# A two-block transformer forward pass on one core: moving modulation work, key casts, one early expert block and the table's side products

## What is computed

```python
def first_block(x, mem, ...):       # layer 0: h @ l0_w_in ("even_in"), mixers, @ l0_w_out ("even_out")
    ...                             # layer 1: h @ l1_w_in ("odd_in"), mixers, @ l1_w_out ("odd_out")

def second_block(x, c, ...):
    for l in range(DEPTH):                                     # DEPTH = 2
        mod = (silu(c) @ ada_w[l] + ada_b[l])[:, None, :]      # 6 * 1024 values
        sh1, sc1, g1, sh2, sc2, g2 = jnp.split(mod, 6, axis=-1)
        h = rmsnorm(x, norm_mix_g[l]) * (1.0 + sc1) + sh1
        y = rglru_block(h, ...) if l == 0 else mla_block(h, ...)
        x = x + g1 * y
        h = rmsnorm(x, norm_ffn_g[l]) * (1.0 + sc2) + sh2
        x = x + g2 * peer(h, peer_w_q[l], peer_sub_keys[l], peer_u[l], peer_v[l])

def peer(h, w_q, sub_keys, u_tab, v_tab):                      # 8 heads, 128 * 128 experts
    q = (h @ w_q).reshape(B, S, 8, 2, -1)
    s = einsum('bshpd,hpnd->bshpn', q, sub_keys)
    v1, i1 = top_k(s[..., 0, :], 16);  v2, i2 = top_k(s[..., 1, :], 16)
    cv, ci = top_k(all 16 * 16 sums of v1 and v2, 16)
    idx = i1[ci // 16] * 128 + i2[ci % 16];  g = softmax(cv)
    act = gelu(h . u_tab[idx]);  return sum(g * act * v_tab[idx])
```

## Time and profile before

| | before |
|---|---|
| median of 3 runs | 2448.44 us (2446.98 to 2449.4) |
| profiled execution | 2445.76 us, span 2444.5 us, mean granted clock of PE 0.992 |
| PE, PEld | 2355.5 us (96%), 1923.0 us (79%) |
| DVE, ACT, POOL | 1914.9 us (78%), 1164.6 us (48%), 154.2 us (6%) |
| `even_in` products begin | 45.54 us |
| `odd_out` second half, up to the next stage's first transposes | 425 to 446 us |
| routing of layer 0, DVE's last instruction | 662.95 us |
| table of layer 0, first and last store on ACT | 670.59 us, 755.73 us |

### The profile page before, as it was taken

One profiled execution on the slowest core, in us unless ns is written; L12 is line 12 of the kernel. 1 busy time (PEld: TensorE's weight loads), 2 busy tenths in 40 slices (PEclk: granted clock), 3 DMA queues, 4 the chain that ended last, 5 costly groups with the idle time before them and its releaser, 6 DMA issues. The chain is left out here.

```text
span 2444.5 us, 37915 instructions
## 1 busy us (share of the span) xinstructions
PE 2355.5 (96%) x11759; PEld 1923.0 (79%) x11759; DVE 1914.9 (78%) x4354; ACT 1164.6 (48%) x2035; POOL 154.2 (6%) x172
## 2 busy tenths in 40 slices
PE   7999999999999999999999999999899999999997
PEld 5776466778787888888888877788788888888886
DVE  5677788857997788888888867699877777777776
ACT  5674247242286544444444446316744444444443
POOL 1000000000351000000000000015400000000000
PEclk9999999999999999999999999999999999999999
DMA  7524640653213677777677751311155555555553
GB/s 257 190 102 137 236 170 5 236 197 132 78 36 122 231 252 257 253 253 260 252 253 255 257 187 70 127 63 53 62 193 191 192 193 190 190 189 189 189 189 138
DMA packets 144614, 429.31 MB, mean 176 GB/s; under 512 B 15230, under 2 KB 21374, under 8 KB 144510
## 3 DMA queue, kind: packets, MB, share of 16 engines
q1 hardware_dynamic: 144510, 428.08, 50.0%
HBM read 426.99 MB, written 1.05 MB: 175 GB/s over the span
## 5 line engine op out<-in xcount | busy, mean ns | idle before, releaser
L3405 PE MATMUL bank<-v_parts,weighted_high 128*128 128x512 f32 x1952 | 528.7, 392 | 0.5 <-DVE weighted_low L3548 0.5
L3391 PE MATMUL bank<-h_t_parts,u_t_high 128*128 128x512 f32 x1824 | 450.6, 389 | 0.0
L3405 PEld LDWEIGHTS bank<-v_parts,weighted_high 128*128 128x128 f32 x1952 | 351.1, 189 | 65.6 <-issue 2.6
L3391 PEld LDWEIGHTS bank<-h_t_parts,u_t_high 128*128 128x128 f32 x1824 | 342.3, 188 | 71.3 <-DVE u_t_low L3523 0.3
L3469 ACT ACTIVATE u_t_high<-u_ring 128x1024 fp32r<-128x1024 f32 x228 | 242.0, 1061 | 179.6 <-DMA u_ring<-in_peer_u 178.0
L3488 ACT ACTIVATE activated<-activated 128x256 f32<-128x256 f32 x228 | 95.6, 419 | 474.1 <-DVE activated L3536 474.1
L3523 DVE TENSOR_TENSOR u_t_low<-u_ring,u_t_high 128x1024 fp32r<-128x1024 f32 x228 | 278.7, 1222 | 29.4 <-ACT u_t_high L3469 26.6
L3405 PE MATMUL bank<-v_parts,weighted_low 128*128 128x512 f32 x976 | 301.5, 390 | 0.0
L3530 DVE TENSOR_TENSOR v_parts<-v_ring,v_parts 128x1024 fp32r<-128x1024 f32 x242 | 294.4, 1216 | 3.3 <-ACT v_parts L3476 3.3
L3476 ACT ACTIVATE v_parts<-v_ring 128x1024 fp32r<-128x1024 f32 x242 | 255.1, 1054 | 52.5 <-PE bank L3405 51.7
L3394 PEld LDWEIGHTS bank<-h_t_parts,u_t_low 128*128 128x128 f32 x1824 | 248.8, 190 | 17.8
(11 more groups left out here) (600 smaller groups left out, 3579.8 us busy)
## 6 DMA issues: line engine op xcount, KB each, us to landing
v_ring<-in_peer_v SPq DMA_DIRECT2D x244, 512.0 KB, 3.4
u_ring<-in_peer_u SPq DMA_DIRECT2D x228, 512.0 KB, 4.6
panel<-in_l_w_in SPq DMA_DIRECT2D x15, 2048.0 KB, 8.2
late_tiles<-in_ada_w SPq DMA_DIRECT2D x54, 512.0 KB, 4.3
mod_ring<-in_ada_w SPq DMA_DIRECT2D x42, 512.0 KB, 4.6
panel<-in_peer_w_q SPq DMA_DIRECT2D x8, 2048.0 KB, 7.8
panel<-in_l_w_out SPq DMA_DIRECT2D x4, 2560.0 KB, 10.2
early_u<-in_peer_u SPq DMA_DIRECT2D x20, 512.0 KB, 3.3
```

The lines of the kernel that those rows point to most:

```text
L3391: nc.tensor.matmul(banks[2 + k][:, :], UTH[:, k, j, :], H2[:, j, :, :].rearrange("p a s -> p (a s)"), start=(j == 0), stop=False, skip_gro ...
L3405: last = nc.tensor.matmul(banks[4 + 2 * t + half][:, :], w[:, t * P:(t + 1) * P], v[k][:, half * 512:(half + 1) * 512], start=opens and n ...
```

## The change

1. `even_in`: the first slice isn't split. PE multiplies it unsplit, without the two dummy products before it, and ACT and DVE begin with the second slice.
2. `odd_out`: `mod_steps` becomes (0, 0). Its eight modulation adds go to the end of the LRU stage, behind the second scans and the two `GROW` copies, which move there as well; their loads stand on SP between the second and third output panels. `DIAG` is made after `decays(0)`, and PE's row product stands behind `("gel", 2)`.
3. Routing, both layers: the eight casts of key numbers go from DVE to ACT (`copy_keys`); ACT's list has head h's after the scores of head h + 2, head 6's before the early blocks' copies, head 7's after four of these. POOL waits for the cast on ACT. The tenth early block's products and copy leave the stage (its load stays).
4. Table, both layers: the tenth early block's eight products stand at the head instead of the two dummy products; the 32 side products are spread over 48 steps (none, one, one); in every fourth step POOL makes token 2's one-hot too and DVE doesn't; ACT is fully unrolled, with the copy of the V tile at step 60.

The diff, cut:

```diff
@@ even_in, DVE and ACT (w_high, w_low now count from slice 1) @@
+                    if q:
+                        dve.wait_ge(w_high, q)
...
@@ even_in, PE @@
-                keep_streaming(acc_bank(g0), 2)
...
+                    if q == 0:
+                        wait_panel(pe, ps[0])
+                        for t in range(NT):
+                            last = nc.tensor.matmul(acc_bank(g0 + t)[:, :], HT[:, 0, t * P:(t + 1) * P], slots[ps[0] % 3][:, 0:512],
+                                                    start=True, stop=False)
+                        last.then_inc(used, 1)
+                        continue
@@ odd_out @@
-                     at_dve={0: dve_gated, 1: dve_mean, 2: dve_scale, 4: dve_conv}, mod_steps=(0, 16), plain=2)
+                     at_dve={0: dve_gated, 1: dve_mean, 2: dve_scale, 4: dve_conv}, mod_steps=(0, 0), plain=2)
@@ LRU stage, SP @@
                 modulation.load(sp, 6)
+                load_panels(sp, outs[1] + 1)
+                modulation.load(sp, 16)
                 load_panels(sp, outs[1] + 3)
@@ LRU stage, PE @@
-                    if job == ("rec", 0):
+                    if job == ("gel", 2):
                         pe.wait_ge(diag_ready, 1)
@@ LRU stage, DVE (MOD add and DIAG: from the start to behind decays(0)) @@
                 states(1)
+                for i in range(2):
+                    dve.wait_ge(row_ready, i + 1)
+                    f(v.tensor_copy(GROW[:, i * 512:(i + 1) * 512], banks[4 + i][:, :]), row_stored, wait=False)
+                modulation.add(f, dve, 16)
                 gain_work([(1, sc2, C("norm_ffn_g_2", 0, 8))], 24, 40)(f)
@@ routing @@
+                        if n == ROUTED - 1:
+                            break
...
+                    def copy_keys(h):
+                        act.wait_ge(keys_done, h + 1)
+                        nc.scalar.activation(IDF[:, h, :, :, :].rearrange("p i t k -> p (i t k)"),
+                                             IDX[:, h, :, :, :].rearrange("p i t k -> p (i t k)"), ACT.Copy).then_inc(keys_copied, 1)
...
+                        if g >= 2:
+                            copy_keys(g - 2)
+                    copy_keys(H - 2)
                     for n in range(ROUTED - 2):
+                        if n == 4:
+                            copy_keys(H - 1)
                         copy_early(n)
@@ table @@
+            POOL_TWO = 1
+            spread = KD * (EARLY - ROUTED)
+            last_step = 3 * S // 16
+            early_in = lambda n: n * spread // last_step
...
-                        for u in range(ACT_TOKENS, POOL_TOKEN):
+                        for u in range(ACT_TOKENS, ACT_TOKENS if s == POOL_TWO else POOL_TOKEN):
...
-                        pe.wait_ge(pool_hot, n + 1)
+                        pe.wait_ge(pool_hot, n + 1 + (n + R4 - POOL_TWO) // R4)
...
-                    keep_streaming(banks[7], 2)
+                    for k in range(KD):
+                        last = nc.tensor.matmul(banks[7][:, 0:S], UE[:, head % 3, k * P:(k + 1) * P], HT[:, k, :],
+                                                start=(k == 0), stop=(k == KD - 1))
+                    last.then_inc(head_acted, 1)
```

More of the change, by code:

```diff
@@ L1873, in _ @@
                         wait_used(act, q - 4)
-                    w = slots[ps[i] % 3][:, k * 512:(k + 1) * 512]
-                    nc.scalar.activation(ring[:, q % 4, 0, :], w, ACT.Copy).then_inc(w_high, 1)
+                    if q:
+                        w = slots[ps[i] % 3][:, k * 512:(k + 1) * 512]
+                        nc.scalar.activation(ring[:, q % 4, 0, :], w, ACT.Copy).then_inc(w_high, 1)
                     if k == 2 and i > 0:
@@ L2814, in _ @@
                 conv(0)
-                for i in range(2):
-                    dve.wait_ge(row_ready, i + 1)
-                    f(v.tensor_copy(GROW[:, i * 512:(i + 1) * 512], banks[4 + i][:, :]), row_stored, wait=False)
                 modulation.add(f, dve, 4)
@@ L2826, in _ @@
                 modulation.add(f, dve, 2)
+                f(v.tensor_tensor(MOD[:, 16:24], MOD[:, 16:24], C("ada_b_2", 16, 8), ALU.add))
+                f(v.tensor_tensor(DIAG[:, :, :], ident[:, :].unsqueeze(1).broadcast_to([P, KD, P]),
+                                  g1.unsqueeze(2).broadcast_to([P, KD, P]), ALU.mult), diag_ready)
                 mults(0)
@@ L2971, in _ @@
                     f(nc.scalar.activation(gates, gates, ACT.Exp), exp_out)
-                    for n in range(ROUTED - 2, ROUTED):
-                        copy_early(n)
+                    copy_early(ROUTED - 2)
                 @block.gpsimd
@@ L3102, in _ @@
                             done["cand"] = issued_so_far()
-                        if keys:
-                            dve.wait_ge(dve_order, done["keys"])
-                            dve.wait_ge(keys_done, h + 1)
-                            f(v.tensor_copy(IDF[:, h, :, :, :].rearrange("p i t k -> p (i t k)"),
-                                            IDX[:, h, :, :, :].rearrange("p i t k -> p (i t k)")), wait=False)
-                            done["keys"] = issued_so_far()
                         if h >= 4:
@@ L3169, in peer @@
             table_acted, table_copied = sem(f"peer{l}_table_acted"), sem(f"peer{l}_table_copied")
+            head_acted, head_copied = sem(f"peer{l}_head_acted"), sem(f"peer{l}_head_copied")
+            head = ROUTED - 1
             ACT_TOKENS = 2
             POOL_TOKEN = 3
+            POOL_TWO = 1
+            spread = KD * (EARLY - ROUTED)
+            last_step = 3 * S // 16
+            early_in = lambda n: n * spread // last_step
+            early_end = [next(n for n in range(last_step) if early_in(n + 1) == KD * (b + 1)) for b in range(EARLY - ROUTED)]
             def at_least(eng, s, value):
@@ L3202, in step @@
                         tok = slice(4 * n, 4 * n + 4) if type(n) is int else bass.ds(4 * n, 4)
-                        nc.vector.tensor_tensor(O2[:, s, :, :], rows.broadcast_to([P, 4, P]),
-                                                slot_e2[:, tok].unsqueeze(2).broadcast_to([P, 4, P]), ALU.is_equal)
-                        for u in range(ACT_TOKENS, POOL_TOKEN):
+                        last = nc.vector.tensor_tensor(O2[:, s, :, :], rows.broadcast_to([P, 4, P]),
+                                                       slot_e2[:, tok].unsqueeze(2).broadcast_to([P, 4, P]), ALU.is_equal)
+                        for u in range(ACT_TOKENS, ACT_TOKENS if s == POOL_TWO else POOL_TOKEN):
                             last = nc.vector.tensor_scalar(O1[:, s, u, :], row, slot_e1[:, token(n, u)],
@@ L3225, in _ @@
                                                 ALU.is_equal, ALU.mult).then_inc(pool_hot, 1)
+                        if n % R4 == POOL_TWO:
+                            tok = slice(4 * n + ACT_TOKENS, 4 * n + ACT_TOKENS + 1)
+                            nc.gpsimd.tensor_scalar(O1[:, n % R4, ACT_TOKENS, :], iota[:, :], slot_e1[:, tok], slot_g[:, tok],
+                                                    ALU.is_equal, ALU.mult).then_inc(pool_hot, 1)
                 @block.tensor
@@ L3247, in _ @@
                                     pe.wait_ge(table_copied, b - 1)
+                                elif b:
+                                    pe.wait_ge(head_copied, 1)
                             last = nc.tensor.matmul(banks[6 + b % 2][:, 0:S], UG[:, b % 2, k * P:(k + 1) * P], HT[:, k, :],
@@ L3272, in _ @@
                     nc.scalar.activation(stats[:, 56 + l:57 + l], ident[:, 0:1], ACT.Gelu)
-                    unrolled = KD * (EARLY - ROUTED) + 4 * R4
-                    for n in range(1, unrolled):
+                    for n in range(1, S // 4):
                         gate(n, n % R4)
+                        if n == 1:
+                            act.wait_ge(head_acted, 1)
+                            nc.scalar.activation(ACTED[:, head, :], banks[7][:, 0:S], ACT.Copy).then_inc(head_copied, 1)
                         store(n - 1, (n - 1) % R4)
-                        if n == unrolled - R4:
+                        if n - 2 in early_end:
+                            copy_table(early_end.index(n - 2))
+                        if n == S // 4 - R4:
                             act.wait_ge(v_loaded[0], 16)
                             nc.scalar.activation(VH[0], VR[:, 0, :], ACT.Copy).then_inc(v_high, 1)
-                        if n % KD == 1 and 0 < n // KD <= EARLY - ROUTED:
-                            copy_table(n // KD - 1)
-                    with act.Fori(unrolled // R4, S // 16) as i:
-                        for s in range(R4):
-                            gate(R4 * i + s, s)
-                            store(R4 * i + s - 1, (s - 1) % R4)
                     store(S // 4 - 1, R4 - 1)
```

22 lines of the change are left out of this document (10 added, 12 removed).

## The result

The changed kernel took 2430.25 us (median of 4 runs, 2428.85 to 2430.97) against 2447.71 for the one before (median of 4, 2446.87 to 2449.4); the ratio is 0.993, with a 95% interval of 0.9918 to 0.9942. The profiled executions, whose spans are 2427.6 and 2444.5, differ by 16.9, and this difference can be followed stage by stage.

A forecast was written before the change was run, and what follows sets the result against it. PE, busy 96% of the span, was taken as the bound, with other engines limiting it locally. Terms -6.7 - 1.0 + 0.4 - 2.4 - 2.1 + 0.9 + 0.6 = -10.3 from 2445.76 gave 2435.5, plus 2.7: 2438 us, range 2432 to 2443.5.

The forecast's parts named there:

- odd_out, -6.7: Second half of odd_out: without adds DVE keeps up, PE's wait and half clock go, PE ends 6.7 us earlier.
- even_in, -1.0: Start of even_in: the unsplit first slice runs at once, and the second starts about 1.0 us earlier.
- a gap of 2 or more costs its length and then some 2.6 to 3.4 at half rate: PE anywhere: after such an idle gap the half-rate stretch costs another 1.3 to 1.7 us.
- LRU, +0.4: LRU stage: moved adds fit DVE's idle time; waiting for the gel panel costs 0.4 us, between 0 and 0.9.
- The rival that the adds give back what `odd_out` gained: LRU stage's end: moved adds wait for tiles behind 2 MB panels, total only -6.3 us, 2442; chance 0.16.
- Routing, -2.4 and -2.1: Routing, layers 0 and 1: DVE loses casts, PE stops 2.7 us then runs half rate; stages end 2.4 and 2.1 earlier.
- The part of DVE alone, -3.3 and -3.0: Routing, layers 0 and 1: moving the casts shortens DVE's own list by 3.3 and 3.0 us.
- The heirs of POOL's wait: Routing on DVE: two two-input instructions behind removed casts take over the wait for POOL; without this, -4.4 us.
- Table, +0.9 and +0.6: Table, layers 0 and 1: a longer head outweighs the steps' gain of 1.1, costing 0.9 and 0.6 us.
- at half rate for the first eight or nine, about 5.3: Table's head: the sixteen instructions take about 5.3 us, so the first store comes 2.0 us later.
- The first rival, that the clock doesn't fall and PE isn't late: Routing and table's head: full clock, DVE ends the routing, total -15.8 us, 2432.6; chance 0.17.
- POOL as a limit: Table's steps: POOL's five one-hots per four steps become the bound, 2464 us at 1.2 each; chance 0.04.

The follow-up runs named there:

- e_odd: Kernel before with only the eight modulation adds, the gate's diagonal, row product and copies moved: 2440.32 us against 2447.14.
- e_plain: Kernel before with only the first slice of even_in left unsplit, without its two dummy products: 2446.84 us against 2447.14.
- after_again: The changed kernel timed and profiled a second time, nothing altered: 2430.22 us against 2446.58 for the kernel before.
- a_order: Changed kernel with ACT's cast of head 6 behind two early copies instead of ahead of the first: 2434.35 us.
- e_head: Kernel before with only the tenth early block moved to the table's head, in place of the two dummy products, both layers: 2450.98 us against 2447.14.
- e_head_warm: Kernel before with the tenth early block at the table's head, plus ten dummy products behind the routing's nine blocks: 2447.69 us against 2446.58.
- e_keys_head: Kernel before with only the casts moved to ACT and the tenth early block moved to the table's head, both layers: 2442.16 us against 2446.58.
- k_table: Kernel before with only the table's steps changed in both layers, the head keeping its two dummy products: 2444.19 us against 2447.35.
- a_order_ten: Changed kernel with head 6's cast behind two early copies, the tenth block back in the routing and two dummies at the table's head: 2428.00 us.
- e_keys: Kernel before with only the eight casts moved to ACT in both layers, the tenth block staying in the routing: 2446.63 us against 2447.14.
- a_ten: Changed kernel with the tenth early block back in the routing and the two dummy products back at the table's head: 2434.74 us.

## Why the prediction was wrong, point by point

*odd_out, -6.7.* Right: -6.7 in the trace for the second half (20.31 to 13.61), -6.85 in e_odd with the stages ahead of it. DVE was the limit, and both the 3.31 of waiting and the half clock went.

*even_in, -1.0.* Right for what the change does (1.0). The trace shows 2.0 since in the profiled execution of before the clock fell behind the gap of 1.95 and in that of after it didn't. The step "a gap of 2 or more costs its length and then some 2.6 to 3.4 at half rate", drawn from two gaps, holds for the 3.31 (behind 3.2 to 3.9 it fell in all seven traces that have this gap) and is a matter of chance at 1.95 and at 2.66.

*LRU, +0.4.* Too small to be seen (e_odd above). Up to the output products PE takes 0.17 more in the changed kernel, and then the border to the next stage is 0.35 shorter (0.45 of PE's idle time in place of 0.79), which makes the -0.2. That border is 0.45 in all seven traces with the unsplit first slice, e_plain's among them, and 0.79 to 0.80 in the seven without it, so it comes with the edit of `even_in` and not with this one; why stays open. The rival that the adds give back what `odd_out` gained had the waits (6.5 us for tiles) and not the price.

*Routing, -2.4 and -2.1.* Right in its steps and in size: stop 2.66 for 2.7, -2.4 and -2.2. Half of that is luck, since the lower clock behind the stop was taken as certain and came in 6 of 10 such routings, by chance in both layers here. Its price was right: counted from the stage's first transposes PE's list ends at 102.19 with the fall and at 100.51 without (after_again, layer 1), 1.7 for 1.65. Only 0.5 to 0.7 of it reaches the stage's end, behind DVE. The part of DVE alone, -3.3 and -3.0, is seen in a_order: -3.1 and -2.7. The heirs of POOL's wait show in the trace of after, as two sums of two SBUF inputs, beside POOL's product (584.55 to 586.91) and without one:

```profile
586.39 0.82 DVE L3041 TENSOR_TENSOR candidates<-key_values 128x128 f32<-128x128 f32 x2
...
606.34 0.44 DVE L3041 TENSOR_TENSOR candidates<-key_values 128x128 f32<-128x128 f32 x2
```

The rule of the Trainium skill (SBUF — State Buffer, Who interferes with whom), by which a DVE instruction with two SBUF inputs contends with a GpSimd instruction that reads SBUF, agrees with these rows and with the size: -3.1 is near the 3.3 with heirs, and not the 4.4 without.

*Table, +0.9 and +0.6.* Here the prediction failed. The steps were 84.07 for 84.05. The failed step is "at half rate for the first eight or nine, about 5.3", from which "the first store comes at 672.6 in place of 670.59". It took the clock of the head from the trace of before, where PE had idled 4.32 ahead of it, although the sum's own routing term had PE work up to the stage's end. The 5.3 itself is no bad price for a head at half clock (5.22 in a_order, 5.98 in e_head); the condition for it was gone. Without that idle time the clock is 1.00, the transposes take 0.6 in place of 1.06 and the sixteen instructions 3.69: the head is 0.4 and 0.1 shorter than before in place of 2.0 and 1.7 longer. With 0.2 in layer 1's steps that is 4.4 of the 6.6 us that the sum missed. That it was the clock and no other property of the head, e_head, e_head_warm and a_order show: behind 3.9 and more of idle time all twelve heads were at half clock, behind 0.9 and less all eleven at full clock, and dummies that fill the idle time cured it in one layer of two. Between these the idle time alone doesn't decide (last section).

*The rest* of the miss is 1.0 of chance in `even_in`, 0.6 in the LRU stage with its border, 0.5 at the other borders and 0.1 in the routing. The first rival, that the clock doesn't fall and PE isn't late, came nearest in time, 2432.6, with only half of its mechanism: PE was late and its clock fell in the routing, but the head was warm. POOL as a limit was excluded by the steps, at 1.33 each for the whole stage. The base of 2448.44, 2.7 above the profiled execution, was 0.7 to 1.9 too high, since the other medians of before lie at 2446.58 to 2447.71.

The parts tried alone, e_plain -0.3, e_odd -6.8, e_keys_head -4.4 and k_table -3.2, sum to -14.7, the whole to -17.5 and -16.4. With an error of about 2 for each part, no interaction beyond that of casts and head has to be sought, and none is excluded.

## What to carry to other kernels

Price a moved piece of PE's work with the clock that it will meet, and work that out from the changed schedule: first who ends the stage ahead and how long PE then idles, and then the rate. Two edits that lose or gain nothing apart (+3.8 and -0.5) can gain together (-4.4) if one delays PE just as much as the other relieves it; a stop of PE in the middle of a stage in which another engine is about as late costs little, and to remove it can cost more (a_order, +4.1). Where stages differ by 1 us, compare the durations of stages in the traces, not medians, and over several traces: one gap of 1.95 made `even_in` look twice as good as it was.

## What the hardware showed that I had not expected

The granted clock behind one and the same gap isn't reproducible: after 1.95 of idle time it fell in 7 of 14 executions, for 1.08 us each, after 2.66 in 6 of 10 routings. At the table's heads, by PE's idle time ahead of the transposes, it stayed at 1.00 after 0.91 and less (eleven heads) and after 1.78 (two: after_again and e_keys_head, layer 1), and fell after 1.2 to 1.3 with another 0.65 to 0.81 behind the transposes (three: a_order_ten, and e_head_warm in layer 0). After 3.9 and more the head's products were at 0.50 every time (twelve), though in e_plain's layer 1 the transposes were still at full clock. So the length of the gap alone doesn't tell. The Trainium skill (TensorE: Matmul & The Clock Gate, Part 1: The HAM clock gate) has the activity watched in windows that run free of the kernel. By it, whether a given gap counts would be a matter of phase, which fits these rows; no run here shows such a window.

A fall in the routing's stop costs PE 1.7. Where PE ends the stage that is its whole price (104.69 against 106.38, e_keys and a_ten); where DVE is nearly as late it is 0.5 to 0.7 (102.8 to 103.0 against 102.3).
